# Moving three half turns of an expert-row stream and ScalarE's Gelu within a transformer step on one core

## What is computed

```python
p = rmsnorm(x, ln1) @ w_in                       # q, k, v of two attentions, forget gate, two gates
ya = band attention over chunks; yb = forgetting attention
m = sigmoid(ga) * (ya @ w_br_a) + sigmoid(gb) * (yb @ w_br_b)
h = x + m @ w_out
q = rmsnorm(h, ln2) @ w_pq                        # 8 heads x 2 halves against 128 keys each
idx, gate = best 16 of the product keys, softmax  # 8 x 16 = 128 experts a token, of 16384
a = sum_d peer_u[idx] * rmsnorm(h, ln2)
y = h + sum_k gelu(a) * gate * peer_v[idx]
```

## Time and profile before

| what | value |
|---|---|
| time, median of 3 runs | 2780.39 us (2779.47 to 2781.14) |
| profiled execution | 2781.42 us, its span 2779.5 us |
| mean granted TensorE clock | 0.876 |
| TensorE busy | 2161.4 us (78%) |
| VectorE busy | 1855.5 us (67%) |
| ScalarE busy | 534.6 us (19%) |
| GpSimd busy | 1248.6 us (45%) |
| DMA | 1047.17 MB, mean 377 GB/s |

### The profile page before, as it was taken

How to read it: one execution, slowest core, us unless ns; L and a number is a source line. 1 busy time by engine, 2 the same in 40 slices (tenths; PEclk the granted TensorE clock), 3 DMA queues, 4 the chain that set the end, 5 groups by cost and what they waited for, 6 DMA issues and landing times.

```text
span 2779.5 us, 20637 instructions
## 1 busy us (share of the span) xinstructions
PE 2161.4 (78%) x6540; PEld 1105.8 (40%) x6540; DVE 1855.5 (67%) x2636; ACT 534.6 (19%) x1243; POOL 1248.6 (45%) x858
## 2 busy tenths in 40 slices
PE   7999999999999998888899943340340049999997
PEld 3544444444545443333344443330330035444443
DVE  1222001677687866667576899999999997666666
ACT  1222000112222211001001111112994052000000
POOL 2000000135354535535353377777777866454454
PEclk9999999999999999999999976665555568999998
DMA  9887899889899999999999999999999998999999
GB/s 363 325 319 280 278 308 309 319 339 398 326 409 403 407 354 413 406 387 412 409 399 351 412 399 421 421 421 401 400 403 415 422 333 319 409 402 409 408 405 354
DMA packets 271470, 1047.17 MB, mean 377 GB/s; under 512 B 19857, under 2 KB 19857, under 8 KB 203281
## 3 DMA queue, kind: packets, MB, share of 16 engines
q0 software_dynamic: 113792, 697.85, 62.1%
q1 hardware_dynamic: 154880, 343.97, 34.1%
q10 hardware_dynamic: 2704, 4.21, 0.4%
HBM read 1036.50 MB, written 9.45 MB: 376 GB/s over the span
## 4 chain that ended last, share of the span: by engine, by line
PE 39%; DMA 30%; DVE 17%; POOL 7%; issue 5%; ACT 1%; SPq 0%; DVEq 0%; POOLq 0%; ACTq 0%
PE ps L621 35%; DMA yTr<-in_peer_v,fold 11%; DVE bigr L1717 5%; DMA bigs<-in_peer_u,fold 5%; DMA bigr<-in_w_br_a 3%; DVE hr L1748 3%; POOL bigr L592 3%; DMA bigr<-in_w_in 3%; DMA bigr<-in_w_out 2%; DMA bigs<-in_peer_v,idxnow 2%; DMA bigr<-in_peer_v,fold 2%; POOL bigs L592 2%; DVE bigs L1717 2%; DVE spare L1717 1%; POOL spare L592 1%
## 5 line engine op out<-in xcount | busy, mean ns | idle before, releaser
L621 PE MATMUL ps<-bigr 128*128 128x512 f32 x1920 | 852.0, 601 | 39.9 <-DMA bigr<-in_w_in 15.8
L621 PEld LDWEIGHTS ps<-bigr 128*128 128x128 f32 x1920 | 364.7, 193 | 486.2 <-issue 445.4
L541 POOL DMA_INDIRECT bigs<-in_peer_u,idxnow x128 | 225.7, 1763 | 552.1 <-DVE bigs L1656 534.3
L621 PE MATMUL ps<-bigr,bigs 128*128 128x512 f32 x896 | 404.8, 606 | 22.8 <-DMA bigr<-in_w_in 19.2
L1748 DVE SCALAR_TENSOR_TENSOR hr<-yTr,fold,hr 128x1024 f32<-128x1024 f32 x205 | 263.2, 1284 | 135.2 <-DMA yTr<-in_peer_v,fold 134.0
L1646 DVE SCALAR_TENSOR_TENSOR bigs<-bigs,acts 128x2048 f32<-128x2048 f32 x128 | 300.8, 2350 | 62.8 <-DMA bigs<-in_peer_v,idxnow 62.4
L1656 DVE SCALAR_TENSOR_TENSOR bigs<-bigs 128x2048 f32<-128x2048 f32 x128 | 293.0, 2290 | 74.4 <-DMA bigs<-in_peer_u,idxnow 73.3
L602 POOL DMA_INDIRECT yTr<-in_peer_v,fold x205 | 219.2, 1069 | 202.9 <-DVE hr L1748 190.8
L1717 DVE SCALAR_TENSOR_TENSOR bigr<-bigr 128x2048 f32<-128x2048 f32 x122 | 275.9, 2288 | 5.8 <-DMA bigr<-in_peer_u,fold 5.2
L592 POOL DMA_INDIRECT bigr<-in_peer_u,fold x122 | 237.3, 1945 | 51.4 <-issue 35.5
L621 PEld LDWEIGHTS ps<-bigr,bigs 128*128 128x128 f32 x896 | 169.7, 194 | 225.1 <-issue 219.9
(11 more groups left out here) (276 smaller groups left out, 2245.7 us busy)
## 6 DMA issues: line engine op xcount, KB each, us to landing
bigr<-in_w_in SPq DMA_DIRECT2D x160, 1024.0 KB
spare<-in_peer_v SPq DMA_DIRECT2D x96, 512.0 KB
bigr<-in_w_out SPq DMA_DIRECT2D x32, 1024.0 KB
bigr<-in_w_pq SPq DMA_DIRECT2D x32, 1024.0 KB
bigr<-in_w_br_a SPq DMA_DIRECT2D x16, 1024.0 KB
bigr<-in_w_br_b SPq DMA_DIRECT2D x16, 1024.0 KB
bigr<-in_peer_v SPq DMA_DIRECT2D x32, 512.0 KB
bigr<-in_ckT_a POOLq DMA_DIRECT2D x2, 2048.0 KB, 10.2
```

Of the source, the lines that this page charges most:

```text
L541: pool.indirect_dma_start(row, None, table[:, :], bass.IndirectOffsetOnAxis(ap=col, axis=0)).then_inc(loaded, 16)
L621: last = mm(ps[:, bank + t, :], src[:, k0 + k, t * P:(t + 1) * P], wring[:, s, k, :], start=(k0 + k == 0), stop=(k0 + k == kt - 1))
```

## The change

In the passes the counts change from 4, 7, 7, 7 half turns to 6, 6, 6, 7. Ahead of the first pass's first products VectorE now does three half turns (27, 28, 29) instead of one; ahead of those of the other passes three instead of four; behind the sum of the last pass three instead of two. ScalarE's Gelus follow by lines 1115 to 1117. In the groups, ScalarE's Gelus for the third and fourth place (j = 0 and 1) now come before copy_y(j) instead of after it. The instructions are the same in number and kind; VectorE's order in the groups is untouched.

```diff
-PASS_HALVES = ((1, 1, 2), (4, 1, 2), (4, 1, 2), (4, 1, 2))
+PASS_HALVES = ((3, 1, 2), (3, 1, 2), (3, 1, 2), (3, 1, 3))
@@ -1085,9 +1085,10 @@
                         copy_probs(j)
                         if F.streams and j:
                             place_y(H0 + j - 1)
+                        if j + 2 < HC:
+                            experts(HALVES[G][2 + j])
                         copy_y(j)
                         if j + 2 < HC:
-                            experts(HALVES[G][2 + j])
                             exps(j + 2)
```

## The result

| | before | after |
|---|---|---|
| median of 20 runs each | 2779.89 us (2773.06 to 2783.29) | 2783.73 us (2777.84 to 2793.71) |
| ratio, 95% interval | 1 | 1.0019 [1.0011, 1.0027] |
| profiled execution, its span | 2779.5 us | 2784.8 us |

The change makes the kernel slower by 0.19%, some 5 us, where 10.6 us less were forecast. The time lies outside the range. Lines of kernel.py behind 1088 are one higher than before: 1637 is now 1638, 1478 is 1479, 1494 is 1495. Where the text names a line, it is that of the kernel before; rows of a profile have the number of their own kernel.

What follows compares the result with a forecast made beforehand. From the first gate pass to the output's end, time was bytes at 412 GB/s plus what the DMA engines were not asked for. Terms -9.8 + 2.4 - 2.3 - 0.9 = -10.6 us gave 2770 us, range 2761 to 2780.

Steps and rivals of the forecast that it cites:

- The bound and the currency: From first gate pass to output's end, time is bytes at 412 GB/s plus what the DMA engines were not asked for.
- The first pass: Three half turns ahead of the first products close the 1010 to 1030 us hole, 4.0 MB, saving 9.8 us.
- the first join: Second pass's first products: VectorE done near 1113, TensorE near 1118; cost counted as nothing.
- its own formula: At joins, with k pieces in the ring at the start, VectorE waits (4.5-k) x 6.9 us; before, 3.4-k.
- The join with the third pass: Third pass's first products: a wait of 14 to 22 us, costing 4 to 11 us, taken as 6.5.
- The stand on the copies: Before the fourth output piece TensorE stands 9 us for ScalarE's place_m(3) copies; costed at 0, bounds 0 and 9.
- The last products: Last products of the passes come some 20 us earlier, with the output's end only 11 us earlier.
- The length of the output: From last products to last output sum, bytes make 133.2 + 10.2 - 2.3 = 141 us.
- The Gelu order: In the groups, Gelus ahead of the value copies remove three waits, 11.3 us in all; worth -0.9 us.
- A: Rival: gain handed back at joins, two of three opening holes of 4 to 11 us; about 2777 us, chance 0.17.
- B: Rival: slower, the late place_m costing its 9 us in full, plus holes at joins; about 2787 us, chance 0.10.
- rival D: Nothing moves: stream fed earlier, weights starve as much earlier, TensorE's chain sets the end; 2780 us, chance 0.05.

Runs made afterwards that it cites:

- e4: Changed kernel with half turns (3,1,2), (4,1,2), (4,1,2), (2,1,2), the two moved forward taken from the last pass; 2776.67 us, 0.9990 of before.
- e7: Changed kernel with half turns (3,1,2), (4,1,2), (3,1,2), (3,1,2), four again in the second pass; 2772.48 us, 0.9981 of before.
- e11: e7 with ScalarE's Gelu split around the Sigmoids changed for passes starting on an even half turn; 2775.42 us, 0.9987 of before.
- e9: Changed kernel with half turns (2,1,2), (3,1,2), (4,1,2), (4,1,2), one moved forward from the second pass; 2779.68 us, 1.0002 of before.
- e12: e9 with ScalarE's Gelu split around the Sigmoids changed for passes starting on an even half turn; 2776.36 us, 0.9990 of before.
- e3: Changed kernel with ScalarE's copies of the last mix (place_m(3)) ahead of the last Gelu of the passes; 2777.79 us, 0.9995 of before.
- e1: Changed kernel with the half turns of before, so only the Gelu ahead of the value copies differs from before; 2779.70 us, 1.0001 of before.
- e5: Changed kernel with half turns (2,1,2), (4,1,2), (4,1,2), (3,1,2), only one moved forward, from the last pass; 2767.00 us, 0.9963 of before.
- e8: e5 with the Gelu order of the kernel before in the groups; 2769.33 us, 0.9963 of before.

## Why the prediction was wrong, point by point

- **The bound and the currency were right.** The stretch is counted in bytes at 412 GB/s: the kernels with few missing bytes are the fast ones, from 6.7 us at 0.9963 to 25.7 us at 1.0019. As a sum it is loose, since the bytes moved within the stretch differ from kernel to kernel by up to 8.7 us (450.0 to 458.7).
- **The first pass was right in each step.** Gelu at 1006.91 (forecast 1006.1), first products at 1030.01 (near 1030), second at 1042.9 (about 1045), the hole left with 391 GB/s: 8.7 of the 9.8 us were recovered, and TensorE did not wait for the products.
- **The step that failed is the first join**, that with the second pass, where the text says "VectorE done near 1113, TensorE near 1118", "I count nothing". VectorE was done at 1110.2, TensorE at 1135.1: a wait of 24.90 us and a hole of 20 x 244/412 = 11.8 us. The text gives no count of pieces for the 1118. By its own formula the 1118 is too early: the wait of 1.26 us at this join before the change is k = 3.2, and with five half turns (4.5 - 3.2) x 6.9 = 9 us, even with the ring as full as before.
- **What the runs show there in its place** has two parts. The larger is the half turn that the second pass gave away: with six half turns between the passes VectorE is idle 8.5 to 14.0 us there and no hole opens, even where three half turns stand ahead of the first products (e4, e7, e11); with five it is idle 18.9 to 24.9 us and holes of 5.8 to 11.8 us open, even where only one was moved forward (e9, e12). The smaller is the ring. Before, TensorE did eleven pieces without a wait; with three half turns ahead of the first products it did six, its first wait for weights came at 1050.99 instead of 1085.58, and from 1071.76 to 1119.35 it got one per 11.9 us. No kernel has one half turn ahead of the first products and five behind them, so the two parts can't be told apart to the microsecond.
- **The pace behind VectorE's end.** The formula let TensorE run at 6.9 us a piece as soon as VectorE is done. It did not: VectorE was done at 1110.2, but TensorE's next piece began only at 1119.35, 9.2 us on, after a wait of 4.91 us for weights, while the DMA engines ran at their full rate (409 and 406 GB/s from 1110 to 1120). That they were busy with row gathers still queued is the likely reason, and not shown.
- **The join with the third pass**, the second of the text, was forecast at a wait of 14 to 22 us and 6.5 us of bytes; it is 15.48 us and 10 x 189/412 = 4.6 us. That with the fourth pass, counted at nothing, waits 17.83 us and misses 1.2 (316 GB/s from 1335 to 1340).
- **The stand on the copies was found but priced at nothing.** Forecast 9 us within the time of the bytes; it is 17.42 us, since TensorE was at the place 12 us sooner than the text had it (1365.0 for 1376.9, which is the time of the kernel before), and the copies only 3.5 us sooner. The hole behind it is 10 x 250/412 = 6.1 us. e3 takes the stand away and 6.7 us with it; of the bounds 0 and 9 the value taken was the wrong end. That the bytes would cover it failed in two terms: they needed 134 us from the last products to the last output sum (e3), not 141, and TensorE needed 104 us for the 13 pieces behind the stand (1382.44 to 1486.52), not 92.
- **The sum.** Forecast missing bytes 7.6 us, measured 25.7. The parts make 11.8 (join with the second pass) + 6.1 (output) + 1.2 (fourth pass) + 1.0 (left of the first hole) - 1.9 (third pass) = 18.2 of the 18.1 between. In time it is less clear. e7, which takes away the hole at the second pass and the stand, is 0.0038 x 2780 = 10.6 us faster than the change. e3 takes away the stand alone, 6.7 us; the 3.9 us that are left for the join are within the intervals.
- **The last products** came 4.1 us earlier than before (1343.58 for 1347.65), where the text has "some 20 us earlier". So in time 16 of the 17 us between the forecast end of the output (11 earlier) and the measured one (5.7 later) arose ahead of them.
- **The length of the output was right for the wrong reason**, and that is luck: from the last products to the last sum 142.9 us, forecast 141. e3 shows that without the stand it would be 134, so a stand left out and bytes counted too high cancelled.
- **The Gelu order**: waits gone as forecast, worth -0.9 us forecast; e1's 0.0001 [-0.0012, +0.0014] is 0.3 us, between -3.3 and +3.9, so 0.9 could not be seen.
- **The rivals.** A and B had the mechanism, with the wrong join and too little chance: two holes of 11.8 and 6.1 us opened for 8.7 and 2.3 that closed. I put A and B together at 0.27 and argued against A that a long wait fills the ring, so that the next wait is short. The ring does fill: from 1119.35 TensorE did eleven pieces without a wait. But the next wait was still 15.48 us, and the one after it 17.83. And the argument says nothing of the first join, which has no such wait ahead of it once the change has taken it away. In rival D the 110 GB/s for the weights came from mean packets of the whole kernel; see the last section.

What stays open: the price in time of the hole at the second pass by itself; why the join with the third pass has long waits with six half turns ahead of it too (14.69 us before, 18.44 in e9, 19.30 in e4); the 19.93 us ahead of e12's first output sum; and why e1's median is no better than that of before while its profiled stretch is 4.5 us shorter, beyond the scatter of single executions.

## What to carry to other kernels

An idle stretch of the DMA engines is only free if no other queue is catching up in it: before moving demand into one, count what the other consumer's buffers hold at its start and end. Move half as much, and look where the work is taken from: one half turn moved forward from the last pass gave 0.37% (e5, e8), the same half turn taken from the next pass gave nothing that can be told (1.0002 and 0.9990 in e9 and e12), and two gave 0.19% at best (e7) and cost 0.19% the way the change moved them. Of a step whose cost is bounded by 0 and 9 us, and that stands on a chain between two engines, the price should be taken from the top until the cover is worked out with the same care as the rest.

## What the runs showed of the hardware

With both queues full, a piece of 1.049 MB came per 11.7 us before the change (1085.58, 1097.33, 1109.08), 90 GB/s, and per 11.9 us after it, which leaves some 320 of 412 for the row gathers. The queue of the row gathers (q0) and that of the weights (q1) moved the same number of packets then. Before the change, DMA view from 1060 to 1110 us, packets, MB and share:

```profile
q0 software_dynamic: 2222, 16.24, 78.6%
q1 hardware_dynamic: 2233, 4.43, 23.4%
```

After the change it is 2232 and 2236 in the same window. That is what one packet of each in turn would give, with the sizes of this stretch: 7.3 KB and 2.0 KB make the share of the weights 21%, 89 GB/s. The 27% and 110 GB/s that the prediction weighed took the mean sizes of the whole kernel, 6.1 and 2.2 KB.

The stand of TensorE also has a price in its clock. In the window of the stand the granted clock is at the lower of its two levels, 0.50 of full speed (1.2 GHz):

```profile
1370.00:1380.00 10.00, 0.00 (x0) 0.00 (x0) 6.66 (x5) 0.00 (x0) 7.22 (x5) 0.50 1.02 414
```

and it is still there from 1382 to 1385, with TensorE at work again; the five pieces from 1382.44 on took 36.27 us, where five at 6.9 us are 34.5. Of the pieces after waits for weights many took 8.83 us instead of 7.1 (1050.99 and 1071.76 above): during the piece of 1050.99 the granted clock was 0.81, during the next, 7.13 us long, 1.00. While bytes bound the stretch this should be hidden; no run tests it.
